# A second level of block products over pairs of column groups in the up projections

## The chip, the cores and the metric

The kernel runs on one core of a Trainium2 chip. The metric is device time in microseconds (us), the median of three runs. Engines are named as in the profile: PE is TensorE (PEld its weight loads), DVE is VectorE, ACT is ScalarE, POOL is GpSimd, SP is SyncE, which here only issues transfers.

## The reference, cut to what matters

One decode step over 512 prompt tokens and 32 sampled tokens (T = 544 columns), float32 throughout, with two mixer layers and, behind each, this feed-forward layer (D = 1024, D_FF = 4096):

```
def conv_ffn(h, buf, w_up, conv_w, conv_b, w_down):
    T = h.shape[1]
    u = h @ w_up
    full = jnp.concatenate([buf.astype(u.dtype), u], axis=1)
    c = conv_b + sum(conv_w[j] * full[:, j:j + T] for j in range(CONV_W))
    y = jax.nn.gelu(c[..., :D_FF], approximate=True) * c[..., D_FF:]
    return y @ w_down, full[:, T:]
```

The change is in `h @ w_up`, 1024 x 8192 weights in each of the two layers.

## The kernel before

The up projection is cut into 32 groups (FU). Group g makes 128 columns of the value half and the 128 columns of the gate half that belong to them, for all 544 tokens. Weights (as stationary operand) and tokens are 2 x 2 blocks: the two column halves by the two halves of the 1024 inputs (a11, a12, a21, a22, each 512 inputs x 128 columns), and the inputs by the two token halves of 272 columns (b11, b12, b21, b22). Instead of eight block products the group makes seven in the Strassen-Winograd form. Each takes four matmuls (128 inputs each) of 128 x 272, and each float32 matmul stands in the trace as two MATMUL records with a weight load each, so that a product is 8 records and a group 56.

The seven products are named 0 to 6 in the code, by `bank(j)`: 0 is a11 b11, 1 is s3 t3, 2 is the sum a21 + a22 times t1, 3 is a12 b21, 4 is s2 t2, 5 is a22 t4, and 6 is s4 b22. The s are sums of weight blocks, the t sums of token blocks (token_sums, once a layer). From group 4 on (BY_DMA) a21 + a22 (`first_sums`, L4263) and s3 (`third_sums`, L4269) are made by accumulating transfers that POOL issues, and DVE makes only s2 and s4 (`weight_sums`, L3967 and L3969, 128 x 512 each).

Each product goes to a PSUM bank of its own, (7g + j) % 8, in turn. ACT copies products 0, 1 and 2 out (L3496), and DVE adds the rest to them in five steps: `middle` (L4035, the first gate half), `inner` (L4043 to L4047, then two instructions of second_half, L4024 and L4026), and `late` (L4056 and second_half). Then come the convolution over three tokens, whose newest tap ACT makes (`newest`, L3481) and whose other two DVE adds (`convolved`, L4072, four instructions a group), the gelu on ACT (L3486) and the product with the gate (`gated`, L4084 and L4085).

The order on every engine is written out by hand, and semaphores join them. Two groups (2s and 2s + 1) are a pair: they share two 1 MB slots of a ring of four, one with 256 value columns (ka), one with 256 gate columns (kg). SP loads both slots of pair s + 1 (L2686) when pair s - 1 has ended, first ka, then kg. When ka has landed POOL issues its accumulation into itself (L4263). SP also loads the base of s3 (L2676) when its buffer has come free, and POOL issues the accumulation (L4269).

The down projection follows with the same seven products in another loop, on the same helper line L3069. The attention output projection (out_group, L3008) before the first layer already uses token quarters, 136 columns a matmul.

## Time and profile before

| | |
|---|---|
| median of 3 runs | 2111.07 us (2109.31 to 2111.26) |
| time of the profiled execution | 2114.76 us |
| its span in the trace | 2113.0 us |
| PE busy | 2072.9 us, 98% |
| DVE / ACT / POOL busy | 1282.7 us (61%) / 641.3 us (30%) / 301.5 us (14%) |
| granted TensorE clock, mean | 0.995 |

The profiled execution lasts 2114.76 us, of which the trace spans 2113.0 us. PE is busy nearly all the time, the other engines are not, so idle time of theirs costs nothing as long as PE doesn't wait for them. A page of the profile tells busy shares over the whole span; what one stage is like is read from windows and from the timeline.

### The profile page before, as it was taken

The numbers are of one execution on the slowest core, as the hardware profiler recorded it, in microseconds if no ns is written. First come the engines' busy times: TensorE is split into PE (matmuls) and PEld (weight loads), VectorE is DVE, ScalarE is ACT, GpSimd is POOL, SyncE is SP. The second block draws the span as 40 slices with busy tenths as digits, with TensorE's granted clock in tenths as the row PEclk, the third lists the DMA queues.
The fourth block names the chain that finished last, engine by engine and source line by source line (L and its number), as shares of the span: only waits on it lengthen the run. The fifth ranks groups of instructions, "written<-read, shape, count | busy, mean of one in ns | idle before, by whom it ended". The sixth has DMA issues, their size and how long they took to land.

```text
span 2113.0 us, 30884 instructions
## 1 busy us (share of the span) xinstructions
PE 2072.9 (98%) x11286; PEld 1642.7 (78%) x11286; DVE 1282.7 (61%) x3006; ACT 641.3 (30%) x1474; POOL 301.5 (14%) x583
## 2 busy tenths in 40 slices
PE   8999999998899999999999999999999999999998
PEld 7556777787788888888888775778888888888887
DVE  5257996676876666668323784655866666665223
ACT  3016886563332222221001220543322222220002
POOL 1002000000032222221000100410222222220001
PEclk9999999999999999999999999999999999999999
DMA  9228106994256666562221324252365666642223
GB/s 221 60 60 275 49 2 160 281 247 84 80 125 143 145 140 140 140 140 85 88 90 62 134 80 101 71 161 87 108 140 140 146 149 149 148 102 80 80 80 116
DMA packets 270664, 258.21 MB, mean 122 GB/s; under 512 B 42771, under 2 KB 251899, under 8 KB 270003
## 3 DMA queue, kind: packets, MB, share of 16 engines
q1 hardware_dynamic: 232898, 209.13, 34.7%
q0 software_dynamic: 37616, 47.12, 11.6%
q8 instruction: 91, 1.49, 0.3%
q14 instruction: 59, 0.48, 0.1%
HBM read 227.92 MB, written 21.93 MB: 118 GB/s over the span
## 4 chain that ended last, share of the span: by engine, by line
PE 92%; DVE 3%; ACT 2%; DMA 1%; issue 1%; SPq 1%; DVEq 0%; ACTq 0%
PE PS L3069 58%; PE PS L1881 3%; PE PS L2847 2%; PE PS L855 2%; PE PS L2868 2%; PE PS L1673 2%; PE PS L783 2%; PE PS L1752 2%; PE PS L770 2%; PE PS L803 2%; PE PS L1625 2%; PE PS L3008 1%; PE PS L2877 1%; PE PS L843 1%; PE PS L2771 1%
## 5 line engine op out<-in xcount | busy, mean ns | idle before, releaser
L3069 PE MATMUL PS<-HT,ring 128*128 128x272 f32 x1536 | 374.3, 393 | 2.3 <-DVE HT L3995 2.3
L3069 PE MATMUL PS<-arena,ring 128*128 128x272 f32 x1392 | 341.6, 392 | 0.0
L3069 PEld LDWEIGHTS PS<-HT,ring 128*128 128x128 f32 x1536 | 291.8, 190 | 63.4 <-ACT arena L3413 1.8
L3069 PEld LDWEIGHTS PS<-arena,ring 128*128 128x128 f32 x1392 | 264.3, 190 | 54.5
L3481 ACT ACTIVATE arena<-arena,CB,CW 128x560 f32<-128x560 f32 x128 | 109.2, 854 | 377.5 <-DVE arena L4056 313.4
L4072 DVE SCALAR_TENSOR_TENSOR arena<-arena,CW 128x560 f32<-128x560 f32 x256 | 192.7, 796 | 11.8 <-ACT arena L3481 11.8
L3069 PE MATMUL PS<-arena,CONST 128*128 128x272 f32 x768 | 191.7, 392 | 0.0
L3069 PE MATMUL PS<-arena 128*128 128x272 f32 x768 | 191.3, 392 | 0.0
L3069 PEld LDWEIGHTS PS<-arena,CONST 128*128 128x128 f32 x768 | 145.9, 190 | 30.1
L3069 PEld LDWEIGHTS PS<-arena 128*128 128x128 f32 x768 | 145.8, 190 | 30.0
L4288 POOL COPY arena<-arena 128x16 f32<-128x16 f32 x128 | 57.1, 446 | 467.0 <-DVE arena L4056 369.5
L4035 DVE TENSOR_TENSOR arena<-RT,PS 128x272 f32<-128x272 f32 x64 | 28.1, 439 | 137.5 <-PE PS L3069 137.5
L3069 PE MATMUL PS<-HT,arena 128*128 128x272 f32 x384 | 96.8, 395 | 0.5 <-issue 0.5
L3069 PE MATMUL PS<-HT,CONST 128*128 128x272 f32 x384 | 95.8, 392 | 0.0
L3526 ACT COPY RT<-PS 128x272 f32<-128x272 f32 x15 | 5.8, 387 | 273.2 <-PE PS L3069 273.2
L3069 PEld LDWEIGHTS PS<-HT,arena 128*128 128x128 f32 x384 | 73.4, 192 | 16.5 <-issue 1.3
L3069 PEld LDWEIGHTS PS<-HT,CONST 128*128 128x128 f32 x384 | 73.0, 190 | 15.0
L4282 POOL COPY arena<-arena 128x16 f32<-128x16 f32 x128 | 80.9, 915 | 0.1
L3980 DVE TENSOR_TENSOR arena<-ring 128x512 f32<-128x512 f32 x20 | 13.8, 690 | 109.5 <-PE PS L3069 109.5
L4024 DVE TENSOR_TENSOR arena<-RT,PS 128x240 f32<-128x240 f32 x64 | 25.9, 405 | 85.9 <-PE PS L3069 85.9
L1113 ACT ACTIVATE arena<-arena 128x128 f32<-128x128 f32 (+3 forms) x128 | 70.7, 560 | 4.3 <-DVE arena L1267 4.3
L855 PE MATMUL PS<-arena 128*128 128x256 f32 x256 | 67.0, 386 | 2.1 <-DVE arena L1336 1.8
(570 smaller groups left out, 3364.3 us busy)
## 6 DMA issues: line engine op xcount, KB each, us to landing
ring<-in_w_ffn_up SPq DMA_DIRECT2D x64, 1024.0 KB, 6.6
ring<-in_w_ffn_down SPq DMA_DIRECT2D x32, 1024.0 KB, 5.0
ring<-in_cache_nsa_kv SPq DMA_DIRECT2D x128, 128.0 KB, 5.5
arena<-in_cache_nsa_kv SPq DMA_DIRECT2D x56, 256.0 KB, 6.9
ring<-ring POOLq DMA_DIRECT2D x28, 512.0 KB, 7.5
ring<-in_w_ml_in SPq DMA_DIRECT2D x12, 1024.0 KB, 5.4
arena<-in_cache_nsa_win SPq DMA_DIRECT2D x16, 512.0 KB, 7.1
out_nsa_win_sample<-in_cache_nsa_win POOLq DMA_DIRECT2D x8, 1016.0 KB, 17.6
```

The lines of the kernel that those rows point to most:

```text
L770: last = mm(PS[:, 2 * (p % 2) + g2, c0:c0 + w], QT[rows, n, i * P:(i + 1) * P], KTS[rows, br - 1, n // 4, 0:w], start=True, stop=True)
L783: last = tr(PS[:, 4 + g2, k * P:(k + 1) * P], PB[:, u % 6, k * P:(k + 1) * P], ident)
L803: last = mm(out(g2, i), KVP[:, k, c0:c0 + 64], PTS[:, (2 * p + g2) % 4, s0 + k * P:s0 + (k + 1) * P], start=(p % NU == 0 and m == 0), stop ...
L855: last = mm(PS[:, 2 + c, 0:256], W1[:, c, a_, :], CT[:, (16 * n + 8 * b + a_) % 3, :, c, :], start=(a_ == 0), stop=(a_ == 7))
L1113: last = nc.scalar.activation(PB[:, u % 6, cols], SB[:, u % 4, cols], ACT.Exp, scale=-1.0, bias=ST[:, p % 4, 0, m, g2:g2 + 1], accum_out=S ...
L1625: last = mm(PS[:, bank, 0:HALF], lhs[:, k, :], rhs[:, k, :], start=(k == 0), stop=(k == 3))
L1881: last = mm(PS[:, bank, 0:HALF], R[:, r, k, (m % 2) * P:(m % 2 + 1) * P], turned_heads(k)[:, half(h)], start=(k == 0), stop=(k == KT - 1))
L3069: last = mm(PS[:, bank, 0:HALF], lhs[:, k, :], rhs(k), start=(first and k == 0), stop=(done and k == 3))
L3481: nc.scalar.activation(CV[:, 2 * (g % 2) + ag, :], U[:, 2 * (g % 2) + ag, 2:562], ACT.Identity, bias=cb[:, l, n:n + 1], scale=cw[:, l, 2, ...
L4072: v.scalar_tensor_tensor(out=c, in0=U[:, 2 * (g % 2) + ag, tap:tap + 560], scalar=cw[:, l, tap, n:n + 1], in1=c, op0=ALU.mult, op1=ALU.add)\
L4282: g_.tensor_copy(U[:, 2 * (g % 2) + ag, 514:562].rearrange("p (b s) -> p b s", b=NB)[:, :, 0:2], UB[:, n, :].rearrange("p (b r) -> p b r", ...
L4288: g_.tensor_copy(ULS[:, n, :].rearrange("p (b r) -> p b r", b=NB), u[:, 514:562].rearrange("p (b s) -> p b s", b=NB)[:, :, 4:6])
```

## The change

It concerns pairs 2 to 15 of each layer (DEEP), that is groups 4 to 31. Products 0 and 2 of the two groups of a pair are no longer made group by group. For the gate slot (z = 0: a11 of both groups, times b11) and for the value slot (z = 1: a21 + a22 of both groups, times t1) the pair's 512 x 256 block is itself cut into 2 x 2 blocks (256 inputs x 128 columns), the tokens into two quarters of 136, and the seven products of the same form are made from them (`deep_products`): 14 matmuls of 128 x 136 in place of 8 of 128 x 272. A set has its own weight sums, four DVE instructions of 128 x 256 (`deep_sums`, into XT), four token sums once a layer (`deep_tokens`), one ACT copy of 128 x 136 (`deep_copy`), and four DVE additions that join the seven products into the results of both groups (`deep_joins`: three of 128 x 272, one of 128 x 136). The two sets stand ahead of the pair's other products on PE. The other five products of each group follow in the order 3, 1, 4, 5, 6 of the code (in the form's usual numbering the second, seventh, sixth, fourth and third product). ACT's six copies a pair (products 0, 1 and 2 of both groups) go. Every group's u sums are taken straight from PSUM (`deep_part`). XT, which holds the residual stream, is saved to memory and loaded back around the first layer's up projection.

PE, one pair in the steady part, first as it was: products 1 to 5 and the start of 6 of an even group. All rows are products over 272 columns, s_sig30 and s_sig10 are the accumulating transfers, s_su the weight sums, s_ac the copies, s_ev the additions.

```order
L3069 MATMUL PS<-arena 128x272 [waits s_ac,s_sig30]
L3069 MATMUL PS<-arena 128x272 x3
L3069 MATMUL PS<-HT,ring 128x272 [waits s_ac,s_sig10]
L3069 MATMUL PS<-HT,ring 128x272 x3
L3069 MATMUL PS<-HT,ring 128x272 [waits s_ac]
L3069 MATMUL PS<-HT,ring 128x272 x3
L3069 MATMUL PS<-arena 128x272 [waits s_ev,s_su]
L3069 MATMUL PS<-arena 128x272 x3
L3069 MATMUL PS<-arena,ring 128x272 [waits s_ev]
L3069 MATMUL PS<-arena,ring 128x272 x3
L3069 MATMUL PS<-HT,arena 128x272 [waits s_ev,s_su]
L3069 MATMUL PS<-HT,arena 128x272 x3
```

And now, of an even pair, the second set (z = 1) and the products behind it. XT holds the sums of weights and tokens, s_ls says that the weight sums are there, s_lc the joins.

```order
L3149 MATMUL PS<-XT 128x136 [waits s_ls]
L3149 MATMUL PS<-XT 128x136 x5
L3149 MATMUL PS<-HT,XT 128x136 [waits s_ac,s_ls]
L3149 MATMUL PS<-HT,XT 128x136
L3149 MATMUL PS<-XT,ring 128x136 x2
L3107 MATMUL PS<-HT,ring 128x272 [waits s_lc]
L3107 MATMUL PS<-HT,ring 128x272 x3
L3107 MATMUL PS<-arena 128x272 [waits s_sig30]
L3107 MATMUL PS<-arena 128x272 x3
L3107 MATMUL PS<-arena 128x272 [waits s_su]
L3107 MATMUL PS<-arena 128x272 x3
```

Seven small products stand where two large ones of two groups stood, and products 3 and 1 of the even group now come behind both sets.

DVE, as it was, from `inner` of one group over `late` and `convolved` to the weight sums of the next (L3967, L3969).

```order
L4043 TENSOR_TENSOR RT<-RT,PS 128x272 [waits s_pr]
L4046 TENSOR_TENSOR RR<-RR,RT 128x272 [waits s_ac,s_ev]
L4047 TENSOR_TENSOR RT<-RT,arena 128x272
L4024 TENSOR_TENSOR arena<-arena,RR 128x240 [waits s_ev]
L4026 TENSOR_TENSOR arena<-arena,RR 128x8x4
L4056 TENSOR_TENSOR arena<-PS,RR 128x272 [waits s_ev,s_pr]
L4024 TENSOR_TENSOR arena<-RT,PS 128x240 [waits s_pr]
L4026 TENSOR_TENSOR arena<-RT,PS 128x8x4
L4072 SCALAR_TENSOR_TENSOR arena<-arena,CW 128x560 [waits s_c1] x2
L4072 SCALAR_TENSOR_TENSOR arena<-arena,CW 128x560 [waits s_cva] x2
L3967 TENSOR_TENSOR CONST<-ring 128x512 [waits s_ring3,s_pr,s_sig10]
L3969 TENSOR_TENSOR CONST<-ring,CONST 128x512 [waits s_su]
```

DVE now, in the even group of a pair: `deep_part` c11 (L4282), the sums of the next pair's gate slot (L4219 to L4224), and u2 and u3 (L4285, L4289), for which product 6 of the even group waits. s_ring3 is the arrival of that slot.

```order
L4282 TENSOR_TENSOR arena<-RT,PS 128x272 [waits s_ul,s_pr,s_lc]
L4219 TENSOR_TENSOR XT<-ring 128x256 [waits s_lp,s_ring3]
L4220 TENSOR_TENSOR XT<-ring 128x256
L4222 TENSOR_TENSOR XT<-XT,ring 128x256 [waits s_ls]
L4224 TENSOR_TENSOR XT<-ring,XT 128x256 [waits s_ls]
L4285 TENSOR_TENSOR arena<-RT,PS 128x272 [waits s_pr]
L4289 TENSOR_TENSOR RR<-arena,PS 128x272 [waits s_pr,s_ev]
```

Four sums that wait for a slot now stand between c11 and u2.

DVE in the odd group of the same pair, from the end of the even group's c12 (L4128) to u3 of the odd group (L4289). L4237 and L4249 are s2 and s4 of the next pair's even group, s_sig10 the accumulation into that pair's value slot.

```order
L4128 TENSOR_TENSOR arena<-arena,PS 128x8x4
L4219 TENSOR_TENSOR XT<-ring 128x256 [waits s_lp,s_sig10]
L4220 TENSOR_TENSOR XT<-ring 128x256
L4222 TENSOR_TENSOR XT<-XT,ring 128x256 [waits s_ls]
L4224 TENSOR_TENSOR XT<-ring,XT 128x256 [waits s_ls]
L4282 TENSOR_TENSOR arena<-RT,PS 128x272 [waits s_ul,s_pr,s_lc]
L4237 TENSOR_TENSOR arena<-ring 128x512 [waits s_ring3,s_pr,s_sig10]
L4249 TENSOR_TENSOR arena<-ring,arena 128x512 [waits s_pr,s_su]
L4172 SCALAR_TENSOR_TENSOR arena<-arena,CW 128x560 [waits s_c1] x2
L4172 SCALAR_TENSOR_TENSOR arena<-arena,CW 128x560 [waits s_cva] x2
L4285 TENSOR_TENSOR arena<-RT,PS 128x272 [waits s_pr]
L4289 TENSOR_TENSOR RR<-arena,PS 128x272 [waits s_pr,s_ev]
```

The next pair's sums, both weight sums and the convolution of the even group all stand ahead of u2 and u3 of the odd group.

The diff, cut to its core:

```diff
+DEEP = tuple(range(2, FU // 2))
+DEEP_SETS = (1, 2, 6, 7, 5, 3, 4)
+DEEP_ORDER = (3, 1, 4, 5, 6)
...
                 def third_bases(g0):
                     for g in (g0, g0 + 1):
                         c = sum_columns(g) + FF
-                        sp.wait_ge(s_pr, PR0[l] + 7 * (FU * l + g - 2) + 2)
+                        sp.wait_ge(s_pr, deep_done(l, g - 2, 1))
...
+                def deep_products(s, z):
+                    e = deep_set(l, s, z)
+                    w11, w12, w21, w22 = deep_blocks(l, s, z)
+                    s3, s1, s2, s4 = (DS[z][:, n] for n in range(4))
+                    x = HT[:, 0:4, z * HALF:(z + 1) * HALF]
...
+                    for j in DEEP_SETS:
+                        lhs, rhs, bank, half_ = {1: (w11, x[:, 0:2, qa], 0, qa), 2: (w12, x[:, 2:4, qa], 1, qa),
+                                                 6: (s2, t2, 1, qb), 7: (s3, t3, 2, qb), 5: (s1, t1, 2, qa),
+                                                 3: (s4, x[:, 2:4, qb], 0, qa), 4: (w22, t4, 3, qa)}[j]
+                        if j in (6, 3):
+                            pe.wait_ge(s_ls, 4 * e + {6: 3, 3: 4}[j])
+                        if j == 3:
+                            pe.wait_ge(s_ac, deep_copied(l, s, z))
+                        for k in range(2):
+                            last = mm(PS[:, 4 * z + bank, half_], lhs[:, k, :], rhs[:, k, :], start=(k == 0), stop=(k == 1))
+                        last.then_inc(s_lp, 1)
+
+                def deep_group(s, g):
...
+                    pe.wait_ge(s_lc, 4 * e + 3)
+                    product(deep_bank(g, 3), a12, b21, True, True).then_inc(s_pr, 1 if z else 5)
+                    pe.wait_ge(s_sig3[g % 2], third_sum(l, g))
+                    product(deep_bank(g, 1), s3, t3, True, True).then_inc(s_pr, 1)
+                    pe.wait_ge(s_su, su + 3)
+                    product(deep_bank(g, 4), s2, t2, True, True).then_inc(s_pr, 1)
+                    pe.wait_ge(s_lc, 4 * e + 4)
+                    product(deep_bank(g, 5), a22, t4, True, True).then_inc(s_pr, 1)
+                    pe.wait_ge(s_su, su + 4)
+                    pe.wait_ge(s_ev, EV0[l] + 7 * u + 3)
+                    product(deep_bank(g, 6), s4, b22, True, True).then_inc(s_pr, 1)
+
+                def deep(s):
...
+                    if s == DEEP[0]:
+                        pe.wait_ge(s_ac, AC0[l] + 3 * u)
+                        pe.wait_ge(s_ev, EV0[l] + 7 * u)
+                    else:
+                        pe.wait_ge(s_ev, EV0[l] + 7 * (u - 1))
+                    pe.wait_ge(s_lt, 4 * (l + 1))
+                    deep_products(s, 0)
+                    pe.wait_ge(s_sig1[s % 2], first_sum(l, 2 * s))
+                    pe.wait_ge(s_ev, EV0[l] + 7 * u)
+                    deep_products(s, 1)
+                    deep_group(s, 2 * s)
+                    deep_group(s, 2 * s + 1)
...
+                    if l == 0 and k == 3:
+                        sp.wait_ge(s_nrm, normed(1, 1) + 8)
+                        sp.dma_start(hsc[:, :], XTF[:, :]).then_inc(s_xl, 16)
...
+                    if l == 0 and d == 4:
+                        sp.wait_ge(s_xl, 16)
+                        sp.dma_start(XTF[:, :], hsc[:, :]).then_inc(s_xl, 16)
...
+                def deep_sums(s, z):
...
+                    if z == 0:
+                        dve.wait_ge(s_w[up_slots(l, 2 * s)[1] % RING], loaded(up_slots(l, 2 * s)[1]))
+                    else:
+                        dve.wait_ge(s_sig1[s % 2], first_sum(l, 2 * s))
+                    if e >= 2:
+                        dve.wait_ge(s_lp, 7 * (e - 2) + 7)
+                    tt(s3, w11, w21, sub).then_inc(s_ls, 1)
+                    tt(s1, w21, w22, add).then_inc(s_ls, 1)
+                    dve.wait_ge(s_ls, 4 * e + 2)
+                    tt(s2, s1, w11, sub).then_inc(s_ls, 1)
+                    dve.wait_ge(s_ls, 4 * e + 3)
+                    tt(s4, w12, s2, sub).then_inc(s_ls, 1)
...
+                def deep(s):
+                    g0, g1 = 2 * s, 2 * s + 1
+                    if s == DEEP[0]:
+                        late(g0 - 1)
+                        deep_weights(g1, ("s2", "s4"))
+                    else:
+                        deep_part(s - 1, g0 - 1, ("c12",))
+                        deep_weights(g1, ("s4",))
+                    deep_joins(s, 0)
+                    convolved(g0 - 1)
+                    deep_joins(s, 1)
+                    gated(g0 - 1)
+                    deep_part(s, g0, ("c11",))
+                    deep_sums(s + 1, 0)
+                    deep_part(s, g0, ("u2", "u3", "c21", "c12"))
+                    deep_sums(s + 1, 1)
+                    deep_part(s, g1, ("c11",))
+                    deep_weights(g0 + 2, ("s2", "s4"))
+                    convolved(g0)
+                    deep_part(s, g1, ("u2", "u3"))
+                    gated(g0)
+                    deep_weights(g1 + 2, ("s2",))
+                    deep_part(s, g1, ("c21",))
```

## Rows read from the trace of the kernel before

**Rows 1.** The page: busy times, and the granted TensorE clock in 40 slices.
```profile
PE 2072.9 (98%) x11286; PEld 1642.7 (78%) x11286; DVE 1282.7 (61%) x3006; ACT 641.3 (30%) x1474; POOL 301.5 (14%) x583
...
PEclk9999999999999999999999999999999999999999
```

**Rows 2.** The page: the chain that ended last, by engine.
```profile
PE 92%; DVE 3%; ACT 2%; DMA 1%; issue 1%; SPq 1%; DVEq 0%; ACTq 0%
```

**Rows 3.** Windows view, first feed-forward layer: window, busy us (xcount) per engine.
```profile
650.00:940.00 290.00, 290.00 (x1268) 240.41 (x1267) 180.04 (x386) 77.32 (x134) 82.65 (x173) 1.00 0.63 145
```

**Rows 4.** Timeline, PE, one pair: start us, us, engine, line, operation, count.
```profile
797.21 2.00 PE L3069 MATMUL PS<-HT,ring 128*128 128x272 f32 x8
...
822.87 2.00 PE L3069 MATMUL PS<-HT,ring 128*128 128x272 f32 x8
```

**Rows 5.** Timeline, DVE, the first group of that pair.
```profile
797.41 0.41 DVE L4024 TENSOR_TENSOR arena<-RT,PS 128x240 f32<-128x240 f32 x1 [1.39 <-PE PS L3069]
797.73 0.18 DVE L4026 TENSOR_TENSOR arena<-RT,PS 128x32 f32<-128x32 f32 x1
797.83 0.80 DVE L4072 SCALAR_TENSOR_TENSOR arena<-arena,CW 128x560 f32<-128x560 f32 x1
798.83 2.23 DVE L4072 SCALAR_TENSOR_TENSOR arena<-arena,CW 128x560 f32<-128x560 f32 x3 [0.21 <-ACT arena L3481]
800.98 0.68 DVE L3967 TENSOR_TENSOR CONST<-ring 128x512 f32<-128x512 f32 x1
801.69 0.69 DVE L3969 TENSOR_TENSOR CONST<-ring,CONST 128x512 f32<-128x512 f32 x1
804.74 0.44 DVE L4035 TENSOR_TENSOR arena<-RT,PS 128x272 f32<-128x272 f32 x1 [2.36 <-PE PS L3069]
805.10 0.68 DVE L4084 TENSOR_TENSOR arena<-arena 128x512 f32<-128x512 f32 x1
805.70 0.19 DVE L4085 TENSOR_TENSOR arena<-arena 128x32 f32<-128x32 f32 x1
```

**Rows 6.** Timeline, PE, attention output: matmuls over 136 columns.
```profile
532.10 2.94 PE L3008 MATMUL PS<-arena 128*128 128x136 f32 x24
534.88 1.09 PE L3008 MATMUL PS<-HT,arena 128*128 128x136 f32 x8
```

**Rows 7.** Source view, L3008: weight loads, ns min/median/max.
```profile
L3008 PEld LDWEIGHTS PS<-arena x144: 186/190/190, 502.3 to 541.9; 128*128 128x128 f32 x144
```

**Rows 8.** Lines view, DVE, 500 to 545 us: a 136-column addition.
```profile
L3716 DVE TENSOR_TENSOR arena<-arena,PS 128x136 f32<-128x136 f32 x28 | 7.9, 294 | 7.0 <-PE PS L3008 6.8
```

**Rows 9.** Timeline, transfers issued on SP in that pair.
```profile
797.40 0.99 SPq L2686 DMA_DIRECT2D ring<-in_w_ffn_up  x2
801.07 0.37 SPq L2676 DMA_DIRECT2D arena<-in_w_ffn_up  x1
```

**Rows 10.** Source view, L2686: both loads of pairs at 617, 823, 1713 us.
```profile
DMA to landing us min/median/max: 6.4/8.2/10.0
...
DMA to landing us min/median/max: 7.1/9.1/11.2
...
DMA to landing us min/median/max: 5.9/9.2/12.6
```

**Rows 11.** Timeline, 538.3 to 539.7 us: TensorE waits for a DVE result.
```profile
538.88 0.70 DVE L3716 TENSOR_TENSOR arena<-arena,PS 128x136 f32<-128x136 f32 x3
...
539.23 0.73 PE L3008 MATMUL PS<-arena 128*128 128x136 f32 x4 [0.40 <-DVE arena L3716]
```

**Rows 12.** Timeline, POOL, the accumulating transfers of that pair.
```profile
798.75 1.26 POOL L4269 DMA_DIRECT2D CONST<-in_w_ffn_up  x1
804.18 0.87 POOL L4263 DMA_DIRECT2D ring<-ring  x1 [4.17 <-DMA ring<-in_w_ffn_up]
```

**Rows 13.** Source view, L4263, 610 to 945 us: the accumulation into the value slot.
```profile
DMA to landing us min/median/max: 7.4/7.6/8.4
```

More of the change, by code:

```diff
@@ L3093, in ffn @@
                 for g in range(FU):
+                    if g // 2 in DEEP:
+                        if g % 2 == 0:
+                            deep(g // 2)
+                        continue
                     u = FU * l + g
@@ L3471, in ffn, with newest @@
                 cb = CB[:, :].rearrange("p (l c) -> p l c", l=2)
-                def newest(g):
+                def newest(g, parts=(0, 1)):
                     u = FU * l + g
-                    for ag in range(2):
+                    for ag in parts:
                         n = g + 32 * ag
@@ new lines, in deep_weights @@
+                def deep_weights(g, names):
+                    blocks = up_blocks(l, g) if g < FU else down_blocks(g - FU)
+                    a11, a12, a21, a22 = blocks
+                    s2, s3, s4 = (WS[g % 2][:, q] for q in range(3))
+                    n = SU0[l] + 4 * (g + (FU + FD) * l)
+                    for x in names:
+                        if x == "s2" and g < FU:
+                            dve.wait_ge(s_sig1[g // 2 % 2], first_sum(l, g))
+                            dve.wait_ge(s_w[up_slots(l, g)[1] % RING], loaded(up_slots(l, g)[1]))
+                            dve.wait_ge(s_pr, deep_done(l, g - 2, 4))
+                            tt(s2, a21, a11, add).then_inc(s_su, 3)
+                        elif x == "s2":
+                            dve.wait_ge(s_dw[(g - FU) % 3], down_loaded(l, g - FU))
+                            dve.wait_ge(s_pr, deep_done(l, g - 2, 1))
+                            tt(s3, a11, a21, sub).then_inc(s_su, 1)
+                            tt(a21, a21, a22, add).then_inc(s_su, 1)
+                            dve.wait_ge(s_su, n + 2)
+                            dve.wait_ge(s_pr, deep_done(l, g - 2, 4))
+                            tt(s2, a21, a11, sub).then_inc(s_su, 1)
+                        else:
+                            dve.wait_ge(s_su, n + 3)
+                            dve.wait_ge(s_pr, deep_done(l, g - 2, 6))
+                            tt(s4, a12, s2, add if g < FU else sub).then_inc(s_su, 1)
@@ L4090, in ffn @@
+                for g in range(DEEP[0] * 2):
                     if g:
                         late(g - 1)
-                    weight_sums(l, g + 1, 0)
+                    if g + 1 not in BY_DMA:
+                        weight_sums(l, g + 1, 0)
                     if g:
                         convolved(g - 1)
-                    weight_sums(l, g + 1, 1)
-                    if g < FU:
-                        middle(g)
+                    if g + 1 not in BY_DMA:
+                        weight_sums(l, g + 1, 1)
+                    else:
+                        deep_weights(g + 1, ("s2", "s4"))
+                    middle(g)
@@ L4098, in ffn @@
                     if g:
                         gated(g - 1)
-                    if g < FU:
-                        inner(g)
+                    if g == 1:
+                        deep_tokens()
+                    if g == 2:
+                        deep_sums(DEEP[0], 0)
+                    inner(g)
+                deep_sums(DEEP[0], 1)
+                for s in DEEP:
+                    deep(s)
+                deep_part(DEEP[-1], FU - 1, ("c12",))
+                deep_weights(FU + 1, ("s4",))
@@ L4103, in ffn @@
+                convolved(FU - 1)
+                gated(FU - 1)
                 dve.wait_ge(s_y, FU * (l + 1))
```

184 lines of the change are left out of this document (139 added, 45 removed).

## The prediction

> **What bounds the kernel now.** First the page: PE is busy 98% of the span at a granted clock of nearly 1 throughout, DVE 61% [rows 1]. The chain that ended last runs over PE for 92% [rows 2]. The window over the deep part of the first up projection shows PE busy 290.00 of 290.00 us, DVE 180.04 [rows 3]. So here the number and width of the matmuls set the time, and DVE has room as long as nothing that PE waits for comes late. A pair starts at 797.21 and the next at 822.87: 25.66 us for 14 products, 1.833 us each, 0.229 a record [rows 4].
>
> **What PE saves.** A matmul over 136 columns is in the trace: 24 records from 532.10 to 534.88 are 0.1158 us each [rows 6]. A set is 14 matmuls, 28 records, 3.24 us. It replaces 16 records over 272 columns, 3.67 us. That saves 0.42 us a set, and with two sets in 14 pairs of two layers, 56 sets, 23.6 us. A pair would last 24.82 us without waits (two sets 6.49, ten products 18.33). This is the whole gain; the other edits can only take from it.
>
> A rule speaks against even this: the Trainium skill, "TensorE: Matmul & The Clock Gate", section "The mechanism", says that a weight load overlaps running matmuls only where the row group differs. Here all use all rows. The loads last 190 ns [rows 7], yet the records follow each other at 116 [rows 6], so the trace disagrees.
>
> **What DVE gets.** Spacings from the timeline of one group [rows 5]: 272 columns without a dependence 0.36 (804.74 to 805.10), 512 columns 0.60, a split half 0.42 (0.32 and 0.10), one convolution instruction 0.72 (three from 798.83 to 800.98). On a direct dependence the next starts 0.03 after the end (800.98 plus 0.68, then 801.69), so 0.47 for 272 columns and 0.71 for 512. A 136-column addition lasts 0.294 [rows 8]; 256 columns then last 0.42 (estimate, between 0.294 and 0.44), spaced 0.34 or, dependent, 0.46. A set's weight sums are 0.34 + 0.46 + 0.46 + 0.34 = 1.59 us, its joins 0.47 + 0.47 + 0.36 + 0.21 = 1.5. Two sets add 6.2 us a pair to the 15.9 that DVE is busy now (180.04/290 of 25.66): 22.1 of 24.82, 89%. It fits in sum. What counts is the order, and there are two places where PE waits for u3 (L4289), since product 6 reuses the bank that u3 reads.
>
> **Place one: product 6 of the odd group.** I follow DVE from the moment that product 6 of the even group has ended. DVE sees a product 0.20 after the next one starts on PE (797.21 and 797.41 [rows 4, 5]). Then come c12 0.42, sums of the value slot 1.59, c11 0.36, s2 0.71, s4 0.60, the convolution 2.86, u2 0.47, u3 0.44: 7.45, with the 0.20 it is 7.65. PE meanwhile has four products, 7.33. A stalled PE restarts later than the result: the first of DVE's additions starts at 538.88 and ends 0.29 later [rows 8], at 539.17, and PE starts at 539.23, 0.05 for the signal; its four records then take 0.73 [rows 11], where three spacings of 0.116 and the last one's 0.28 are 0.63, so 0.10 for the refill (the last two estimates come from this one place). The stall is 7.65 - 7.33 + 0.15 = 0.48 us a pair. Before, none of this stood between two products, and PE ran through [rows 3].
>
> **Place two: product 6 of the even group.** It is due 13.82 us into the pair (6.49 and four products). Ahead of u3 stand u2 and the four sums of the gate slot, which wait for kg: 1.59 + 0.47 + 0.44 + 0.08 of signals. So kg must have landed by 11.24 us into the pair. DVE itself is ready at 9.1: the first set's joins end 0.4 after the set, at 3.7, then convolution 2.86, joins 1.5, gated 0.70, c11 0.36. The load is issued when the pair before has ended: ka at 797.40, 0.2 into the pair, kg 0.4 later, at 0.6 (both issues take 0.99) [rows 9], and kg lands 10.0 to 12.6 us after issue (maxima of the two loads, [rows 10]). So 10.64 after the issue is the edge: 10.0 is in time, 11.2 is 0.6 late, 12.6 is 1.9 late. Of the 26 loads that gate a pair here, 17 land in time and 9 late (the same view, pair by pair; rows 10 show one early, one typical and the latest of the late ones), 4.8 us together, and with 0.1 of restart each 5.7 us. Now nobody waits for kg at that point: the weight sums that use it come later. The base load L2676, at 3.7 us into the pair now [rows 9], moves to 10.3 (after product 1 of the even group), behind kg as before, so I leave kg's time.
>
> POOL's accumulation into CONST is issued 1.5 us into the pair, while ka and kg run [rows 12], and does so still.
>
> The value slot's accumulation starts 7.0 us into the pair and takes 7.4 to 8.4 [rows 12, 13], so it ends by 15.4; its sums come behind product 6 of the even group, at 16.3 (15.65 + 0.20 + 0.42). Covered by 0.9 us.
>
> **The rest.** In the first deep pair PE waits for all additions of group 3, which DVE reaches after four more sums: 9.37 (product 4 seen) + 1.6 + 1.59 + 0.36, then c12 after product 6, ending at 13.5 against 12.83: 0.87 with the restart, twice, +1.7. In the last pair four weight sums of the down projection replace two (+1.2) but 1.59 of sums go: -0.4 of stall, twice, -0.7. The token sums (four of 544 columns, 2.9 us) lie in group 1, where DVE idles 2.3 us ahead of L4035 alone [rows 5] and PE needs the results only a group later: nothing. Saving and loading XT (2.2 MB each) runs while the ring is loaded ahead by two pairs or groups: nothing. ACT loses four copies a pair: nothing, it was never waited for. What would these cost uncovered: up to 3 us once for the tokens, 10 us once for XT.
>
> **Sum.** Matmuls -23.6, place one 28 x 0.48 = +13.4, place two +5.7, start +1.7, end -0.7: -3.5 us. On the profiled execution, 2113.0 of span and 1.8 around it, that is 2114.8 - 3.5 = 2111.3. It lay 3.7 above the median of 2111.07; the same difference on the median gives 2107.6, and I say 2108 us, a change of 0.15%.
>
> **Bounds.** Both stalls are small differences of long chains. Place one is bounded below by 0 (-13.4) and above by 256 columns costing as 272 each (8 sums, dependent 0.47, spacing 0.36) and an added 0.05 for each of six instructions with several waits: 0.8 a pair, +9. Place two: kg 0.5 us earlier leaves some 2 us, 0.5 later (the same transfers against a shorter pair) costs about 14 us more, since most loads lie near the edge.
>
> **Rivals.**
> 1. DVE keeps up. If the chains are a little shorter or kg comes earlier, the first stall shrinks and the second goes. For it: of the 0.48 of place one 0.15 is restart, measured at one place only. Against it: 7.65 against 7.33 is positive before any restart. With half of place one and none of place two: -23.6 + 6.7 + 1.7 - 0.7 = -16, 2095; with place one whole, 2102. I put 2100 for it. Chance 0.30.
> 2. Slower: the gate slot's arrival sets the pair. Place: the first gate sum (L4219) waits for kg, u2 and u3 of the even group are queued behind it on DVE, and product 6 of the even group waits for u3. Each us that kg lands behind 11.24 is a us on PE, in 26 pairs. It decides from a mean lateness of 0.35 us above what I count (26 x 0.35 = 9 us). For it: loads up to 12.6 are there, and the pair is shorter, so the same bytes come in less time. Against it: 17 of 26 are in time now. At 0.5 later, 2108 + 14 = 2122. Chance 0.31.
> 3. The weight loads bind in a stream of short matmuls: 28 x 0.19 = 5.32 us a set instead of 3.67, +1.65 in 56 sets, +92, 2203. The spacing of 0.116 speaks against it [rows 6]. Chance 0.02. By the rule cited above it would be so.
> 4. The change does not do what it says: the order of instructions shows 28 records where 16 stood, so only a chance of 0.01, with a time as before, 2111.
>
> **Chances and range.** My forecast, small net gain of 1 to 8 us, has 0.36; 2103 to 2115 is its own range. A measurement tells 0.2%, 4.2 us, from no change: faster means below 2106.9. A third of my case and all of rival 1 but little lie there: 0.39. Slower than 2115.3 is most of rivals 2 and 3 with a rest of mine: 0.33. Within: 0.28. The range reaches from 2096, which takes in most of rival 1, to 2127, most of rival 2.
>
> **What the profile after would show.** Sets of 28 records over 136 columns in 3.24 us; if 0.116 a record is wrong, all is. The idle time of PE ahead of product 6 of the odd group, for L4289, 0.3 to 0.5 us in nearly every pair, and in about one pair in three ahead of the even one; DVE idle about 2 us ahead of L4219, released by the ring's transfer; DVE busy 85 to 90%. A pair of 25.3 us where kg is in time. Wrong would be: PE idle elsewhere in the pair (at the joins, or for the value slot), idle of L4219 over 2.5 us, or no idle of PE at all, with pairs of 24.8.

## The result and the profile after

The changed kernel takes 2116.68 us (median of 20 runs, 2111.54 to 2122.59), the kernel before 2112.30 (20 runs, 2109.31 to 2115.65). The ratio is 1.0023, with a 95% interval of 1.0015 to 1.0032: slower by 0.23%. The forecast was 2108, faster by 0.15%. The time lies inside the range, but on the other side of no change.

The profiled execution of the changed kernel lasts 2122.59 us, its span is 2120.8, 7.8 above the span before. It is the slowest of its 20 runs, so sums over this trace come out some us larger than the median shows.

The page after, busy time, share and instructions of each engine, then the chain by engine:

```profile
PE 2059.3 (97%) x11958; PEld 1650.2 (78%) x11958; DVE 1434.5 (68%) x3462; ACT 590.4 (28%) x1362; POOL 275.5 (13%) x583
...
PE 76%; DVE 12%; DMA 5%; issue 3%; ACT 2%; SPq 1%; DVEq 0%; ACTq 0%
```

PE's busy time is 13.6 us less than before [rows 1] and the kernel is longer all the same. That this is not the 23.6 us of the forecast lies mostly in how busy time is counted: it takes in a modelled tail of 0.17 us ahead of each of 34 waits (5.8), a slower start behind each of 42 (0.08 a time, 3.4) and one slow product (1.5), all told of below. The chain, 92% PE before [rows 2], now runs over DVE for 12% and transfers for 5%. The window that answers to [rows 3]:

```profile
650.00:940.00 290.00, 284.32 (x1530) 243.05 (x1528) 237.82 (x564) 56.10 (x89) 71.78 (x168) 1.00 0.63 146
```

PE was busy 290.00 of 290 there and is now idle for 5.68. DVE went from 180.04 to 237.82, 82%: below the 85 to 90% forecast, and far from full. Who PE waits for, as line of PE, line waited for, us in total, times, longest:

```profile
PE PS L3107 <- DVE RR L4289: 18.2, 34, 3.5
```

L3107 issues the products of 272 columns, L4289 computes u3; the records of a deep set stand under L3149. These views count as busy the modelled tail of a matmul (0.17 us). I measure a stall from start to start, less 1.833 for a product, so a stall reads 0.17 larger, and by that measure there are 41: the seven shortest, of 0.16 to 0.22 us, are not in the view's count.

One pair of PE's timeline after, where the gate load came in time. It answers to [rows 4]:

```profile
746.27 1.09 PE L3149 MATMUL PS<-HT,ring 128*128 128x136 f32 x8
...
749.52 1.09 PE L3149 MATMUL PS<-HT,ring 128*128 128x136 f32 x8
...
758.26 2.00 PE L3107 MATMUL PS<-arena,ring 128*128 128x272 f32 x8
760.09 2.00 PE L3107 MATMUL PS<-HT,arena 128*128 128x272 f32 x8
761.93 2.00 PE L3107 MATMUL PS<-HT,ring 128*128 128x272 f32 x8
...
767.43 2.00 PE L3107 MATMUL PS<-arena,ring 128*128 128x272 f32 x8
769.79 2.07 PE L3107 MATMUL PS<-HT,CONST 128*128 128x272 f32 x8 [0.36 <-DVE RR L4289]
771.69 0.51 PE L3149 MATMUL PS<-HT,ring 128*128 128x136 f32 x3
```

A set is 28 records in 3.25 us (746.27 to 749.52), 0.116 each: the saving is as forecast. The pair is 25.42 us (746.27 to 771.69), forecast 25.3. Product 6 of the odd group starts 0.53 late (769.79 - 767.43 - 1.83) and takes 0.07 to 0.08 more itself (771.69 - 769.79 = 1.90). Product 6 of the even group (760.09) does not wait: kg came early enough. DVE in the same pair, the odd group behind product 6 of the even one:

```profile
762.20 0.41 DVE L4126 TENSOR_TENSOR arena<-arena,PS 128x240 f32<-128x240 f32 x1 [1.32 <-PE PS L3107]
...
762.62 0.42 DVE L4219 TENSOR_TENSOR XT<-ring 128x256 f32<-128x256 f32 x1
...
764.22 0.42 DVE L4282 TENSOR_TENSOR arena<-RT,PS 128x272 f32<-128x272 f32 x1
764.57 0.68 DVE L4237 TENSOR_TENSOR arena<-ring 128x512 f32<-128x512 f32 x1
765.28 0.69 DVE L4249 TENSOR_TENSOR arena<-ring,arena 128x512 f32<-128x512 f32 x1
765.89 2.94 DVE L4172 SCALAR_TENSOR_TENSOR arena<-arena,CW 128x560 f32<-128x560 f32 x4
768.74 0.43 DVE L4285 TENSOR_TENSOR arena<-RT,PS 128x272 f32<-128x272 f32 x1
769.20 0.44 DVE L4289 TENSOR_TENSOR RR<-arena,PS 128x272 f32<-128x272 f32 x1
```

DVE idles 1.32 us, sees product 6 of the even group 0.27 us after the next product has started (761.93 and 762.20), then works without a gap from 762.20 to 769.64, 7.44 us, while PE has 7.33. Idle ahead of the stretch and a stall behind it: a matter of order, not of load. Nothing but u2 and u3 in it is needed by PE's next step; s2 and s4 (L4237, L4249) are for the next pair's group.

Added over this trace, by start to start:

| | forecast | measured |
|---|---|---|
| matmuls, 56 sets | -23.6 | -23.6 |
| product 6 of the odd group, usual pair, 26 times | 0.48, +12.5 | 0.53 + 0.08, +15.9 |
| the same in the last pair of a layer, twice | 0.48 - 0.35, +0.3 | 1.67 + 0.08, +3.5 |
| product 6 of the even group | 9 times, +5.7 | 13 times, +10.4 |
| start of the deep part, twice | 0.87, +1.7 | 0.96 + 0.08, +2.1 |
| sum | -3.4 | +8.3 |

The 0.08 is what the product behind a wait takes beyond 1.833 (the refill). The span rose by 7.8, so the table leaves nothing large out. The median rose by 4.4: one late load, told of below, makes 5.2 of the even group's 10.4 in this execution alone.

### The profile page after: what moved, and what is told of

It is laid out like the page before. It is cut to its first block, busy times and chain, and to the rows that moved or that the text cites. A ratio compares the mean times of both kernels' runs of the same rounds, so it can differ in the third digit from the quotient of the medians.

```text
span 2120.8 us, 32863 instructions
## 1 busy us (share of the span) xinstructions
PE 2059.3 (97%) x11958; PEld 1650.2 (78%) x11958; DVE 1434.5 (68%) x3462; ACT 590.4 (28%) x1362; POOL 275.5 (13%) x583
## 4 chain that ended last, share of the span: by engine, by line
PE 76%; DVE 12%; DMA 5%; issue 3%; ACT 2%; SPq 1%; DVEq 0%; ACTq 0%
PE PS L3107 36%; PE PS L3149 6%; DMA ring<-in_w_ffn_up 4%; DVE arena L4172 3%; PE PS L1889 3%; PE PS L2885 2%; PE PS L2906 2%; PE PS L1681 2%; PE PS L791 2%; PE PS L1760 2%; PE PS L778 2%; PE PS L863 2%; PE PS L811 2%; PE PS L1633 2%; PE PS L3046 1%
## 5 line engine op out<-in xcount | busy, mean ns | idle before, releaser
L3107 PE MATMUL PS<-arena,ring 128*128 128x272 f32 x1392 | 341.6, 392 | 0.0
L3107 PEld LDWEIGHTS PS<-arena,ring 128*128 128x128 f32 x1392 | 264.3, 190 | 54.5
L4172 DVE SCALAR_TENSOR_TENSOR arena<-arena,CW 128x560 f32<-128x560 f32 x256 | 188.0, 796 | 0.3 <-ACT arena L3570 0.2
L3107 PE MATMUL PS<-arena,CONST 128*128 128x272 f32 x768 | 187.1, 392 | 0.0
L3107 PE MATMUL PS<-arena 128*128 128x272 f32 x768 | 186.8, 392 | 0.0
L3107 PEld LDWEIGHTS PS<-arena,CONST 128*128 128x128 f32 x768 | 145.9, 190 | 30.1
L3107 PEld LDWEIGHTS PS<-arena 128*128 128x128 f32 x768 | 145.8, 190 | 30.0
L3107 PE MATMUL PS<-HT,ring 128*128 128x272 f32 x640 | 158.9, 393 | 2.3 <-DVE HT L4097 2.3
L3107 PEld LDWEIGHTS PS<-HT,ring 128*128 128x128 f32 x640 | 119.1, 190 | 25.9 <-ACT arena L3502 1.8
L4539 POOL COPY arena<-arena 128x16 f32<-128x16 f32 x128 | 42.7, 333 | 524.6 <-DVE arena L4295 416.8
L3107 PE MATMUL PS<-HT,CONST 128*128 128x272 f32 x384 | 97.9, 398 | 12.7 <-DVE RR L4289 12.7
L3107 PE MATMUL PS<-HT,arena 128*128 128x272 f32 x384 | 98.5, 400 | 6.9 <-DVE RR L4289 5.5
L3107 PEld LDWEIGHTS PS<-HT,CONST 128*128 128x128 f32 x384 | 70.6, 190 | 36.7 <-issue 23.8
L3107 PEld LDWEIGHTS PS<-HT,arena 128*128 128x128 f32 x384 | 72.5, 192 | 27.6 <-issue 13.4
L3575 ACT ACTIVATE arena<-arena 128x560 f32<-128x560 f32 x64 | 43.0, 671 | 180.5 <-DVE arena L4172 180.4
L3149 PE MATMUL PS<-XT 128*128 128x136 f32 x672 | 87.0, 279 | 0.0
L3149 PEld LDWEIGHTS PS<-XT 128*128 128x128 f32 x672 | 82.0, 190 | 0.0
```

Source lines behind the costliest of these rows:

```text
L3107: last = mm(PS[:, bank, 0:HALF], lhs[:, k, :], rhs(k), start=(first and k == 0), stop=(done and k == 3))
L3149: last = mm(PS[:, 4 * z + bank, half_], lhs[:, k, :], rhs[:, k, :], start=(k == 0), stop=(k == 1))
L3575: nc.scalar.activation(CV[:, 2 * (g % 2), :], CV[:, 2 * (g % 2), :], ACT.Gelu_apprx_tanh)\
L4172: v.scalar_tensor_tensor(out=c, in0=U[:, 2 * (g % 2) + ag, tap:tap + 560], scalar=cw[:, l, tap, n:n + 1], in1=c, op0=ALU.mult, op1=ALU.add)\
L4539: g_.tensor_copy(ULS[:, n, :].rearrange("p (b r) -> p b r", b=NB), u[:, 514:562].rearrange("p (b s) -> p b s", b=NB)[:, :, 4:6])
```

## The experiments

The theory: all that was lost is time in which PE waits for u3, and what makes u3 late is where weight sums for later work stand on DVE. The rivals: DVE is simply too full, so that moved work only moves the stall; the other parts of the change (XT saved and loaded back, the tokens' sums) slow the rest, and more work on DVE in that stretch would change nothing; and PE's own handling of its two waits makes the stall. In the quoted texts A stands for the first of these, C for one by which work on DVE is not what counts. Four kernels each were compared with the same 21 runs (2112.18 us; both moves apart and together, the streams) and 17 runs (2111.92; the others) of the kernel before.

### s2 and s4 of the odd group taken out of the way

```diff
                     deep_sums(s + 1, 0)
-                    deep_part(s, g0, ("u2", "u3", "c21", "c12"))
+                    deep_part(s, g0, ("u2", "u3", "c21"))
+                    deep_weights(g1, ("s2", "s4"))
+                    deep_part(s, g0, ("c12",))
                     deep_sums(s + 1, 1)
                     deep_part(s, g1, ("c11",))
-                    deep_weights(g0 + 2, ("s2", "s4"))
                     convolved(g0)
```

The even group's two go behind the joins of its own first set. In the last pair of a layer the four sums for the first group of the down projection go behind `gated`, and so behind u2 and u3 too.

> The changed kernel with one thing moved on DVE: the four instructions s2 and s4 of both groups of a pair no longer stand in the odd group of the pair before (ahead of the convolution and of u2, u3); the even group's stand behind the first set's joins, the odd group's between c21 and c12 of the even group. Theory A (TensorE's saving is whole, 23.6 us, and DVE's order takes it back at two places): the wait of 0.61 us a pair ahead of product 6 of the odd group goes, in 26 pairs, and of 1.75 us in the last pair of each layer: 19 us less than the changed kernel, 2098 us. The wait for the gate slot stays. Theory B (the sets of short matmuls cost more than 0.116 us a record, or DVE is simply full): nothing is gained by an order, 2114 to 2118 us.

Measured: 2104.12 us (2100.60 to 2107.20, 5 runs), ratio to before 0.9962 (0.9948 to 0.9977). Here and below first the line of the waits view, then the rest:

```profile
PE PS L3107 <- DVE RR L4289: 6.7, 10, 2.0
```

```profile
678.62 2.00 PE L3107 MATMUL PS<-arena,ring 128*128 128x272 f32 x8
682.61 2.07 PE L3107 MATMUL PS<-HT,arena 128*128 128x272 f32 x8 [2.00 <-DVE RR L4289]
```

Every wait at the odd group is gone, in the last pairs too. What remains stands ahead of the even group's product 6 (the HT,arena one), 13 times, 9.0 us and 1.0 of refill. Four additions of 512 columns a pair, two of which stood in the stretch ahead of the odd group's u3, moved and not removed, are worth 12.6 us of median against the changed kernel. It is 6 us above what I expected. In this execution the even group's place costs 10.0 where the forecast had 5.7, which would be 4.3 of them; the rest stays open.

### The gate slot's four sums behind c21

```diff
                     deep_part(s, g0, ("c11",))
-                    deep_sums(s + 1, 0)
-                    deep_part(s, g0, ("u2", "u3", "c21", "c12"))
+                    deep_part(s, g0, ("u2", "u3", "c21"))
+                    deep_sums(s + 1, 0)
+                    deep_part(s, g0, ("c12",))
                     deep_sums(s + 1, 1)
```

> The changed kernel with the four sums of the next pair's gate slot moved on DVE from ahead of u2 to behind c21 of the even group, where DVE is idle for about 1.3 us. Theory A: product 6 of the even group waits for nothing any more, the gate slot may land until 14 us into the pair; the waits at this place go, 5 to 10 us in all (10.5 in the profiled execution with one very late load, some 6 in a usual one), so 2110 us; the 0.61 us a pair at the odd group stay. Theory C (the loads' lateness doesn't matter, what DVE does in sum does): no change, 2116 to 2117 us.

Measured: 2110.23 us (2107.76 to 2113.80, 11 runs), 0.9994 (0.9985 to 1.0003).

```profile
PE PS L3107 <- DVE RR L4289: 13.6, 28, 1.5
```

The timeline of DVE in the even group of one pair, then PE around both products 6:

```profile
752.39 0.44 DVE L4285 TENSOR_TENSOR arena<-RT,PS 128x272 f32<-128x272 f32 x1 [3.05 <-PE PS L3107]
...
754.58 0.42 DVE L4219 TENSOR_TENSOR XT<-ring 128x256 f32<-128x256 f32 x1
```

```profile
752.19 2.00 PE L3107 MATMUL PS<-arena,ring 128*128 128x272 f32 x8
754.03 2.00 PE L3107 MATMUL PS<-HT,arena 128*128 128x272 f32 x8
...
761.36 2.00 PE L3107 MATMUL PS<-arena,ring 128*128 128x272 f32 x8
763.76 2.07 PE L3107 MATMUL PS<-HT,CONST 128*128 128x272 f32 x8 [0.40 <-DVE RR L4289]
```

The waits that are left, 28, are those of the odd group; the even one runs through (754.03 - 752.19 = 1.84), since u2 now starts as soon as PE's product is there. The sums at 754.58 hold nobody up. So the two places are two causes, and each edit takes away its own.

### Both

```diff
                     deep_part(s, g0, ("c11",))
-                    deep_sums(s + 1, 0)
-                    deep_part(s, g0, ("u2", "u3", "c21", "c12"))
+                    deep_weights(g1, ("s2", "s4"))
+                    deep_part(s, g0, ("u2", "u3", "c21"))
+                    deep_sums(s + 1, 0)
+                    deep_part(s, g0, ("c12",))
                     deep_sums(s + 1, 1)
                     deep_part(s, g1, ("c11",))
-                    deep_weights(g0 + 2, ("s2", "s4"))
                     convolved(g0)
```

> Both moves together. Theory A: no wait of TensorE is left in pairs 3 to 14, the pair lasts 24.82 us, and the two gains add up: 19 + 6 to 8 us, 2090 to 2092 us. Theory B: 2114 us or more. If the moves only hand the wait on to another place (joins, copy of ACT, the value slot), a pair stays above 25 us and the page names the new place.

Measured: 2089.23 us (2088.31 to 2092.97, 4 runs), 0.9898 (0.9883 to 0.9913) to before, faster by 1.0%. The window of [rows 3], and the pair in PE's timeline:

```profile
650.00:940.00 290.00, 290.00 (x1587) 253.23 (x1586) 249.63 (x586) 61.60 (x94) 89.41 (x179) 1.00 0.62 146
```

```profile
737.79 1.09 PE L3149 MATMUL PS<-HT,ring 128*128 128x136 f32 x8
...
758.94 2.00 PE L3107 MATMUL PS<-arena,ring 128*128 128x272 f32 x8
760.77 2.00 PE L3107 MATMUL PS<-HT,CONST 128*128 128x272 f32 x8
762.61 1.09 PE L3149 MATMUL PS<-HT,ring 128*128 128x136 f32 x8
```

PE is busy 290.00 of 290 again, DVE 249.63 (86%), and the pair lasts 24.82 us, the number of the forecast without waits. The rival of a full DVE falls: it does the same work in less time and is never late. The gain before to here is 23 us, which is the 23.6 of the matmuls less 2.1 at the start (21.5), to 1.5 us. The traces narrow it: from the first to the last record of the feed-forward products of the second layer (L3069 before, L3107 and L3149 here) PE takes 626.30 us before and 615.47 here, 10.8 less, and in the first layer 616.05 against 626.87 in the run of the streams alone (below), 10.8 again: what matmuls and start give is 21.5 / 2. The 1.3 us that are left lie outside these layers. The time is 0.987 of the changed kernel (2089.23 / 2116.68), and none of the other orders tried is faster beyond the noise.

By the medians the two moves apart gain 12.6 and 6.4 us on the changed kernel, 19.0 in sum, and both at once 27.5. In the profiled executions all stalls, from start to start and refills included, add up to 30.9 us in the changed kernel, 11.3 and 21.3 with one move and 1.0 with both, that is 19.6, 9.6 and 29.8 gained: there they add. So the moves take away separate stalls, but why the medians of the single moves gain less is not shown; the even group's wait, which changes from run to run, is part of it.

### Both, and the sums at the start

The value slot's four sums of the first deep pair moved behind the last additions of group 3.

```diff
                     if s == DEEP[0]:
                         late(g0 - 1)
+                        deep_sums(s, 1)
                         deep_joins(s, 0)
```

The call ahead of the loop over the pairs is taken out.

> Both moves, and in the first deep pair of each layer the four sums of the value slot moved from ahead of the last additions of group 3 (late) to behind them. Theory A: the wait of 0.96 us, with 0.08 of refill, at the start of each layer's deep part shrinks to what the last additions of group 3 take behind product 6 (0.2 + 0.42 + signal, at most 0.9 in all), so 0.3 to 1 us less in all than with both moves alone: 2088 to 2089 us, which 5 rounds hardly tell from 2089.2; the trace tells it.

Measured: 2091.19 us (2089.40 to 2091.64, 4 runs), 0.9897 (0.9882 to 0.9911), not to be told from the one before. PE and DVE at the start of the first layer's deep part:

```profile
613.79 2.00 PE L3107 MATMUL PS<-HT,CONST 128*128 128x272 f32 x8
616.58 1.17 PE L3149 MATMUL PS<-HT,ring 128*128 128x136 f32 x8 [0.80 <-DVE arena L4128]
```

```profile
615.82 0.41 DVE L4126 TENSOR_TENSOR arena<-RT,PS 128x240 f32<-128x240 f32 x1 [1.39 <-PE PS L3107]
616.15 0.18 DVE L4128 TENSOR_TENSOR arena<-RT,PS 128x32 f32<-128x32 f32 x1
616.24 0.42 DVE L4219 TENSOR_TENSOR XT<-ring 128x256 f32<-128x256 f32 x1
```

The wait is still 0.96. The four sums stand behind it now and DVE idled 1.39 us ahead of it: my cause for the start was wrong. PE ends product 6 of group 3 at 615.62 (613.79 + 1.83), DVE begins to read it at 615.82 and ends at 616.33, and PE begins the first set only then, since its code waits ahead of the set for all additions of group 3 (`s_ev`, in `deep` above). Product 6 of group 3 lies in bank 3, though, and of the first set only the last of the seven products writes that bank. A wait placed there would let PE begin earlier in this order of the sums; no run tried it. The 0.96 is 0.20 until DVE sees the product, 0.51 for c12 and 0.25 until PE starts, and neither order of the sums changes it.

### The streams alone

The kernel before, with XT saved behind the norm and loaded back in the ring's turn, as the change does; the matmuls and DVE stay.

```diff
+                    if l == 0 and k == 3:
+                        sp.wait_ge(s_nrm, normed(1, 1) + 8)
+                        sp.dma_start(hsc[:, :], XTF[:, :]).then_inc(s_xl, 16)
...
+                    if l == 0 and d == 4:
+                        sp.wait_ge(s_xl, 16)
+                        sp.dma_start(XTF[:, :], hsc[:, :]).then_inc(s_xl, 16)
```

The whole edit also has DVE wait for the loading at the end of the layer, and lets some waits share a semaphore to free one, as the changed kernel does.

> The kernel before with only the saving of the residual stream (2.2 MB out while the first up projection begins, 2.2 MB back in the first down projection) and the wait for it. Theory A, and the prediction: hidden, no change within 1 us. Rival: it delays the ring's loads or the normalisation behind the layer, 2 to 10 us.

Measured: 2112.52 us (2110.07 to 2115.23, 11 runs), 1.0002 (0.9993 to 1.0011). 4.4 MB of added transfers are hidden. The rival of the streams falls for XT; for the tokens' sums and the missing copies of ACT it falls with the version with both moves, which has them and gains in each layer what the matmuls save less the wait at the start.

### PE's two waits exchanged

```diff
-                    pe.wait_ge(s_su, su + 4)
                     pe.wait_ge(s_ev, EV0[l] + 7 * u + 3)
+                    pe.wait_ge(s_su, su + 4)
                     product(deep_bank(g, 6), s4, b22, True, True).then_inc(s_pr, 1)
```

Ahead of product 6 PE waits for two semaphores: s_ev, u3's, which comes last, and s_su, that of s4. In the changed kernel the wait for s_ev stands on an instruction of its own and that for s_su on the first weight load behind it; here it is the other way round.

> The changed kernel with the two waits of product 6 exchanged, so that the wait for u3, which comes last, stands on the weight load itself and the one for the weight sum on an instruction of its own ahead of it. If the wait on an instruction of its own costs TensorE about 0.08 us after the release, each of some 38 waits gets that much shorter: 3 us, 2114 us, near the edge of what can be told; the trace shows the wait at the odd group fall from 0.61 to about 0.53. If not, nothing changes.

Measured: 2113.33 us (2110.59 to 2119.70, 12 runs), 1.0009 (0.9999 to 1.0018) to before, against 1.0023 (1.0015 to 1.0032) for the changed kernel.

```profile
767.10 2.00 PE L3107 MATMUL PS<-arena,ring 128*128 128x272 f32 x8
769.37 2.10 PE L3107 MATMUL PS<-HT,CONST 128*128 128x272 f32 x8 [0.28 <-DVE RR L4289]
771.31 1.09 PE L3149 MATMUL PS<-HT,ring 128*128 128x136 f32 x8
```

The u3 ahead of it on DVE:

```profile
768.88 0.44 DVE L4289 TENSOR_TENSOR RR<-arena,PS 128x272 f32<-128x272 f32 x1
```

PE starts 0.05 after its end (769.32 to 769.37), in the changed kernel 0.15. The wait is 769.37 - 767.10 - 1.83 = 0.44 where it was 0.53, the product's own excess 0.11 (1.94) where it was 0.07: 0.55 against 0.61 in sum, 0.06 to 0.07 a pair. With 28 pairs that is 1.8 us, and the medians differ by 3.4, with intervals that overlap. The times alone so don't tell it from noise, the trace does: the wait order is part of the stall, some 0.06 of 0.61, and not its cause.

### More work in the stretch, in either order

c11 of the odd group (272 columns) cut into eight additions of 34, same result, once in the changed kernel and once in the version with the start's sums moved too.

```diff
-                            tt(ug[:, 2:2 + HALF], p1, ps(3), add).then_inc(s_ev, 1)
+                            n = 8 if g % 2 else 1
+                            w = HALF // n
+                            for i in range(n):
+                                last = tt(ug[:, 2 + i * w:2 + (i + 1) * w], p1[:, i * w:(i + 1) * w],
+                                          ps(3)[:, i * w:(i + 1) * w], add)
+                            last.then_inc(s_ev, 1)
```

> The changed kernel with c11 of the odd group (one DVE addition of 272 columns) cut into 8 pieces of 34 columns with the same result: DVE needs 8 x 0.105 instead of 0.355 us, 0.49 more, in each of 28 pairs, at the place where TensorE waits for u3 of the odd group. Theory A: every us there is a us on TensorE: the wait grows from 0.61 to 1.1, 28 x 0.49 = 14 us, 2130 us. Theory C (only DVE's sum counts; it is 88% busy and has idle time of 1.8 us in the pair): 2117 us.

> The same 8 pieces in the kernel with both moves and the start mended. Theory A: by the moves the chain to u3 of the odd group has some 0.7 to 0.9 us of room, so the extra 0.49 us a pair is hidden: no change against that kernel, 2088 to 2090 us. Theory C: 14 us more, 2103 us.

Measured in the changed kernel: 2131.39 us (2127.21 to 2139.18, 6 runs), 1.0097 (1.0080 to 1.0115) to before. In the other order: 2089.12 us (2087.81 to 2092.93, 4 runs), 0.9887 (0.9873 to 0.9901). The eight pieces in DVE's timeline of the first, then PE's:

```profile
762.94 0.88 DVE L4285 TENSOR_TENSOR arena<-RT,PS 128x34 f32<-128x34 f32 x8
763.74 0.68 DVE L4237 TENSOR_TENSOR arena<-ring 128x512 f32<-128x512 f32 x1
```

```profile
766.14 2.00 PE L3107 MATMUL PS<-arena,ring 128*128 128x272 f32 x8
768.96 2.07 PE L3107 MATMUL PS<-HT,CONST 128*128 128x272 f32 x8 [0.82 <-DVE RR L4294]
```

The pieces take 0.80 (762.94 to 763.74) where the whole took 0.35 (764.22 to 764.57), 0.45 more. PE's stall grows from 0.53 to 0.99, by 0.46, the odd group's stalls of the whole trace from 17.2 to 29.7, and the median by 14.7 us, where 28 x 0.45 would be 12.6; the other 2.1 are not explained. In the other order the same work costs nothing: 2089.12 beside 2091.19. This is the plainest sign of which stretch of DVE sets the time.

## Why the prediction was wrong, step by step

The gain and both places of PE's waits were right. The step that failed is the price of the waits: the hand-overs at place one were taken too short, and the last pair's term subtracted work that turned into idle time, so that the stalls are larger than the gain and the change is slower, not faster.

**What PE saves (-23.6).** Right. A set takes 3.25 us, forecast 3.24, and without waits the pair is 24.82 us to the digit. The rival of binding weight loads is out.

**Place one (0.48 a pair).** The mechanism and the instruction are right, the size too small. The chain that I had added up, 7.45 from c12 to the end of u3, is 7.44 in the trace. What failed are the two hand-overs around it. DVE's first look at product 6 comes 0.27 after the next one has started, where I took 0.20 from one row (762.20 and 761.93 above). And PE starts 0.15 after the end of u3 (769.64 to 769.79), where I took 0.05 from the one restart in [rows 11]; that restart needs one result, here two semaphores are waited for, and with the waits exchanged it is 0.05 again; the refill is longer then, so that 0.06 of the 0.10 is left as a gain. The refill is 0.08, forecast 0.10. 0.07 + 0.10 - 0.01 - 0.02 = 0.14 a pair in these rounded figures; the stalls themselves give 0.13, +3.4 us in 26 pairs. The bound of 0.8 a pair took that in, but for other reasons (dearer sums, and DVE instructions with several waits); the two hand-overs had no spread of their own.

**The end (-0.7).** Wrong in sign: the two last pairs cost 3.5 where two usual ones cost 1.2, so +2.3. I counted what DVE does in the last pair and not what it waits for. PE and DVE there:

```profile
969.91 0.44 DVE L4282 TENSOR_TENSOR arena<-RT,PS 128x272 f32<-128x272 f32 x1 [1.32 <-issue]
...
976.24 0.44 DVE L4289 TENSOR_TENSOR RR<-arena,PS 128x272 f32<-128x272 f32 x1
```

```profile
973.32 2.00 PE L3107 MATMUL PS<-arena,ring 128*128 128x272 f32 x8
976.82 2.07 PE L3107 MATMUL PS<-HT,CONST 128*128 128x272 f32 x8 [1.51 <-DVE RR L4289]
```

With the value slot's sums gone, c11 of the odd group is next on DVE, and it needs product 3 of the odd group: DVE idles 1.32 us ahead of it (the view finds no releaser and says issue). So the 1.59 us that I subtracted become idle time, and the two more sums for the down projection's groups (0.61 and 0.72) come on top in full. From the end of the even group's product 6 (967.82) the chain is 8.86 us (2.09 until DVE starts c11, 0.35 for c11, 2.66 for the four sums of the down projection, 2.85 for the convolution, 0.91 for u2 and u3) against 7.33; with 0.14 until PE starts that is the stall of 1.67.

**Place two (+5.7).** Mechanism and edge right. Compared pair by pair, PE has no stall where kg is there by about 11.0 us after ka's issue, and above that its stall is the excess; I had 11.04 (10.64 and the 0.4 between the two issues). DVE idles ahead of the first sum as forecast, about 2 us; in the pair above:

```profile
757.25 0.42 DVE L4219 TENSOR_TENSOR XT<-ring 128x256 f32<-128x256 f32 x1 [1.84 <-DMA ring<-in_w_ffn_up]
```

That is 10.98 us into the pair, and costs nothing. What failed is above all one load. Late loads were also more frequent than forecast, 13 of 26 and not 9, but twelve of them cost 4.3 us and 0.08 each, 5.3, near the forecast; the thirteenth landed 14.2 us after issue, where the latest before took 12.6 [rows 10]:

```profile
DMA to landing us min/median/max: 5.9/10.0/14.2
```

It cost 5.2 us, of which only 3.65 are wait (see the last section). The size of this place differs from run to run: with the odd group's part moved away it was 10.0 in 13 waits, the longest 2.16. The slower rival, at 2122, named this place, and its condition, lateness 0.35 a pair above mine, was not met: 8.0 us in all against 4.8, 0.12 a pair more.

**Start (+1.7).** The number was near (+2.1), its cause wrong, as the fourth experiment shows, so the number was luck in part. My own sum had it: DVE is through with its list at 9.37 + 1.6 + 1.59 + 0.36 = 12.92, ahead of product 6, seen at 12.83 + 0.20 = 13.03, so the four sums were covered in it already.

**The rest (0).** Right for XT, and by the version with both moves for all else: its layers are shorter by what matmuls and start give, 10.8 us each.

Between the forecast's sum and +8.3 lie 11.7 us: place two 4.7 (the late load), place one 3.4, the last pairs 3.2, the start 0.4. Without the late load the sum is +3.1, beside +4.4 of the medians. So for the medians, which lie 7.9 above the forecast's -3.5, the hand-overs of place one (3.4) and the last pairs (3.2) are most of it, and place two none. A net of -3.5 from 23.6 less 20.1 leaves the sign open to each of these, and those that failed went the same way: hand-overs taken from single rows, an engine's list counted by its work without its waits, and one load later than any seen before.

## What to carry to other kernels

Where one engine works off a list in order, put what the bottleneck needs next ahead of everything that is for later, and look for a place where the list idles just ahead of a stall: moving work there costs nothing, and here it turned +0.2% into -1.0%. When an instruction is taken out of a chain, ask what the next one waits for before the time is counted as won. And a small predicted net that is a gain minus stalls of the same size is best read as the gain plus a list of stalls to remove.

## What the runs showed beside it

A long wait can cost PE more than its length. At 1758.85 the product that had waited 3.65 us took 3.33 to the next start instead of 1.83:

```profile
1753.37 2.00 PE L3107 MATMUL PS<-arena,ring 128*128 128x272 f32 x8
1758.85 3.49 PE L3107 MATMUL PS<-HT,arena 128*128 128x272 f32 x8 [3.49 <-DVE RR L4289]
1762.18 1.08 PE L3107 MATMUL PS<-HT,ring 128*128 128x272 f32 x4
```

Of the granted clock, the window over that product (the column ahead of the last two; the window's us, then busy time of PE, its loads, DVE, ACT, POOL):

```profile
1758.30:1761.80 3.50, 2.95 (x7) 2.28 (x8) 1.53 (x5) 0.85 (x1) 0.31 (x2) 0.51 0.00 0
```

The granted clock was 0.51 in it (1.2 GHz, the lower of its two levels), and 1.00 (2.4 GHz) from 1762.20 to 1765.00. The load of 14.2 us so cost 3.65 + 1.50 = 5.2 us.

The length of the wait alone does not decide it. Behind the wait of 2.16 us at 682.61 (the first experiment) the product takes 2.07 in the timeline as after any short wait. But in the changed kernel with eight pieces it happened behind a shorter one, of 2.12 us, in the last pair, and behind one of 2.33 us at 1764.14:

```profile
978.71 2.93 PE L3107 MATMUL PS<-HT,CONST 128*128 128x272 f32 x8 [1.96 <-DVE RR L4294]
```

The granted clock is 0.50 there from 980 to 983, and the two stretches cost 1.5 and 1.6 us. Profiled executions differ by such stretches, some outside the change: the kernel before has one at 571 us into its trace and a mean granted clock of 0.995, the version with both moves none but at its very end and a mean of 1.000. So spans of two single executions can differ by some us for this alone.

The second is the price of two semaphores ahead of one matmul: 0.15 us from the end of the addition to PE's start with the late one waited for on an instruction of its own, 0.05 with it on the weight load. Since the product behind it then takes 1.94 and not 1.90, some 0.06 a pair is left of the difference.

The 20 runs of the changed kernel scatter over 11 us, the 20 of the kernel before over 6.3, and the 11 with only the gate slot's sums moved, in which PE waits at the odd group but for no load, over 6.0. That fits a time that hangs on when a load lands; no trace of the single runs is there to show it.
